# A GpSimd multiply ahead of the root, and one VectorE instruction per token tile, in the norm stages of a two-block transformer kernel

## What is computed

```python
def rms_norm(x, g):
    xf = x.astype(jnp.float32)
    y = xf * lax.rsqrt(jnp.mean(xf * xf, axis=-1, keepdims=True) + NORM_EPS)
    return (y * g.astype(jnp.float32)).astype(x.dtype)

        x = x + 0.5 * gt1 * rms_norm(swiglu(h, ...), g_post_ffn1[l])
        u = rms_norm(x, g_pre_mix[l]) * (1 + sc2) + sh2
        ...
        x = x + gt2 * rms_norm(y, g_post_mix[l])
        h = rms_norm(x, g_pre_ffn2[l]) * (1 + sc3) + sh3
        x = x + 0.5 * gt3 * rms_norm(swiglu(h, ...), g_post_ffn2[l])
```

## Time and profile before

| | us |
|---|---|
| median of 3 runs | 3116.41 |
| lowest, highest | 3114.98, 3118.16 |
| profiled execution, whole time | 3118.21 |
| profiled execution, span from first to last instruction | 3116.3 |
| mean granted TensorE clock of it, share of full speed | 0.957 |

### The profile page before, as it was taken

The page is one execution under the profiler, slowest core; times in us unless marked ns, Lnnn a source line. Parts: engine busy times, 40 slices in busy tenths (PEclk is TensorE's granted clock), DMA queues, the critical chain, the costliest instruction groups (busy, mean ns, idle before and its releaser), DMA issues. The chain is left out here.

```text
span 3116.3 us, 37658 instructions
## 1 busy us (share of the span) xinstructions
PE 2863.7 (92%) x14102; PEld 2417.8 (78%) x14102; DVE 2013.6 (65%) x3480; ACT 1072.6 (34%) x1575; POOL 923.7 (30%) x614
## 2 busy tenths in 40 slices
PE   4999997987789799997988699999999999999998
PEld 4788885875467688886865579999989999898776
DVE  6773755546842533334535359989588989898887
ACT  1321214224342422223225234655523333333333
POOL 0000000004221000000003134766767777776230
PEclk9999997988899899998998899999999999999999
DMA  7774731200023133331300124566789889888995
GB/s 277 243 255 149 242 122 68 92 26 16 21 68 101 54 108 99 90 101 48 103 13 8 68 84 140 173 191 195 253 330 330 324 327 331 300 335 310 351 348 195
DMA packets 298428, 536.70 MB, mean 172 GB/s; under 512 B 12600, under 2 KB 193180, under 8 KB 280476
## 3 DMA queue, kind: packets, MB, share of 16 engines
q1 hardware_dynamic: 211712, 375.07, 35.3%
q0 software_dynamic: 36864, 134.23, 11.9%
q10 hardware_dynamic: 49692, 25.28, 2.9%
HBM read 495.73 MB, written 38.80 MB: 172 GB/s over the span
## 5 line engine op out<-in xcount | busy, mean ns | idle before, releaser
L173 PE MATMUL ps<-query_h_hi,expert_u_hi 128*128 128x384 f32 (+1 forms) x1152 | 399.6, 347 | 1.9 <-ACT expert_u_hi L2302 1.0
L173 PE MATMUL ps<-query_h_lo,expert_u_hi 128*128 128x384 f32 (+1 forms) x1152 | 395.5, 343 | 0.0
L2041 POOL TENSOR_TENSOR expert_u_lo<-feat,expert_u_hi 128x1024 fp32r<-128x1024 f32 x142 | 349.1, 2460 | 124.2 <-ACT expert_u_hi L2302 122.9
L173 PE MATMUL ps<-expert_v_hi,expert_w_hi 128*128 128x512 f32 x768 | 303.8, 396 | 11.3 <-DVE expert_w_lo L2209 8.7
L173 PE MATMUL ps<-expert_v_hi,expert_w_lo 128*128 128x512 f32 x768 | 301.7, 393 | 0.0
L173 PE MATMUL ps<-expert_v_lo,expert_w_hi 128*128 128x512 f32 x768 | 301.3, 392 | 0.0
L2214 DVE TENSOR_TENSOR expert_v_lo<-peer_s,expert_v_hi 128x1024 fp32r<-128x1024 f32 x128 | 208.2, 1627 | 125.5 <-ACT expert_v_hi L2310 122.6
L173 PE MATMUL ps<-ffn_h_hi,ffn_w_hi 128*128 128x512 f32 x704 | 279.1, 396 | 7.4 <-DVE ffn_h_lo L636 5.8
L173 PE MATMUL ps<-ffn_h_hi,ffn_w_lo 128*128 128x512 f32 x704 | 276.6, 393 | 0.0
L173 PE MATMUL ps<-ffn_h_lo,ffn_w_hi 128*128 128x512 f32 x704 | 276.4, 393 | 0.0
L221 DVE TENSOR_TENSOR ffn_w_lo<-ffn_w_raw,ffn_w_hi 128x2048 fp32r<-128x2048 f32 x66 | 151.1, 2290 | 151.3 <-ACT ffn_w_hi L217 151.3
(11 more groups left out here) (452 smaller groups left out, 6480.7 us busy)
## 6 DMA issues: line engine op xcount, KB each, us to landing
feat<-in_expert_u_blocks SPq DMA_DIRECT2D x64, 1024.0 KB
peer_s<-in_expert_v_blocks SPq DMA_DIRECT2D x64, 1024.0 KB
gate_rows<-expert_gates SPq DMA_DIRECT2D x31, 768.0 KB
ffn_w_raw<-in_w_gate SPq DMA_DIRECT2D x44, 512.0 KB, 4.0
ffn_w_raw<-in_w_up SPq DMA_DIRECT2D x44, 512.0 KB, 5.3
ffn_w_raw<-in_w_down SPq DMA_DIRECT2D x22, 1024.0 KB, 4.9
gate_rows<-in_w_mod SPq DMA_DIRECT2D x18, 1024.0 KB, 6.4
in_w_raw<-in_w_in SPq DMA_DIRECT2D x16, 1024.0 KB, 5.1
```

The lines of the kernel that those rows point to most:

```text
L173: return nc.tensor.matmul(out, lhsT, rhs, start=start, stop=stop, skip_group_check=True)
L2041: nc.gpsimd.tensor_tensor(u_lo[:, n % 2, :, :], u_raw[:, n // 2 % 2, n % 2, :, :], u_hi[:, n % 2, :, :], ALU.subtract).then_inc(u_lo_done, 1)
```

## The change

In the three stages with a post-norm, tiles 1 to 3 get their gate row from GpSimd: `gate_tiles` multiplies `tok` by the row in place, as soon as ScalarE has summed the squares of that tile. VectorE then has one instruction for such a tile in place of two: `tok` times the reciprocal plus the residual, written to the residual. Tile 0 keeps the old pair. ScalarE takes three roots of `tok` up front and not two. A new semaphore, `pool_gated`, tells VectorE that a tile is multiplied.

```diff
+    def gate_tiles(pool):
+
+        for i in range(1, TT):
+            pool.wait_ge(tok_squares, i + 1)
+            nc.gpsimd.tensor_tensor(b.tok[:, i, :], b.tok[:, i, :], b.rows[:, post_row, :], ALU.mult).then_inc(pool_gated, 1)
+
...
+        if post_row is not None:
+            @block.gpsimd
+            def _(pool):
+                gate_tiles(pool)
...
             if post_row is not None:
                 tok_root(0)
                 tok_root(1)
+                tok_root(2)
...
-                if post_row is not None and i + 2 < TT:
-                    tok_root(i + 2)
+                if post_row is not None and i + 3 < TT:
+                    tok_root(i + 3)
...
-                nc.vector.scalar_tensor_tensor(b.tok[:, i, :], b.tok[:, i, :], b.post_stat[:, i:i + 1],
-                                               b.rows[:, post_row, :], ALU.mult, ALU.mult).then_inc(gated, 1)
-                dve.wait_ge(gated, i + 1)
-                nc.vector.tensor_tensor(b.x[:, i, :], b.x[:, i, :], b.tok[:, i, :], ALU.add).then_inc(added, 1)
+                if i == 0:
+                    nc.vector.scalar_tensor_tensor(b.tok[:, i, :], b.tok[:, i, :], b.post_stat[:, i:i + 1],
+                                                   b.rows[:, post_row, :], ALU.mult, ALU.mult).then_inc(gated, 1)
+                    dve.wait_ge(gated, 1)
+                    ins = nc.vector.tensor_tensor(b.x[:, i, :], b.x[:, i, :], b.tok[:, i, :], ALU.add)
+                else:
+                    dve.wait_ge(pool_gated, i)
+                    ins = nc.vector.scalar_tensor_tensor(b.x[:, i, :], b.tok[:, i, :], b.post_stat[:, i:i + 1], b.x[:, i, :],
+                                                         ALU.mult, ALU.add)
+                ins.then_inc(added, 1)
```

More of the change, by code:

```diff
@@ L542, in stage_norm_turn @@
     gated = b.sem(f"{tag}_gated")
+    pool_gated = b.sem(f"{tag}_pool_gated")
     added = b.sem(f"{tag}_added")
```

## The result

| | before | after |
|---|---|---|
| median, us | 3115.21 | 3120.66 |
| lowest to highest, 20 runs each | 3112.83 to 3120.25 | 3117.71 to 3123.83 |
| span of the profiled execution | 3116.3 | 3116.3 |

The changed kernel takes 1.0016 times as long, with a 95% interval of 1.0009 to 1.0023: it is slower by 5.45 us, by the interval 2.8 to 7.2. That is inside the forecast range and on the forecast side, 5 us under the forecast of 3125.7. The profiled execution of after happens to be among its shortest, so its span says nothing; what follows is read inside the stages.

What follows compares the result with a forecast made beforehand. The prediction took VectorE's chain to bound the three stages. It summed 3.5 us for the first stage and 2 x 2.9 for the others to 9.3, on 3116.4: 3125.7 us, range 3119 to 3130.

Steps and rivals of the forecast that it cites:

- VectorE's list is the bound: In the three stages VectorE's 18.47 us chain delays the first evacuation; a microsecond on it is one of the program.
- Exclusion by whole instructions: In the stages, GpSimd's multiplies and VectorE's large two-SBUF-input instructions take turns whole; nothing overlaps.
- The price of a multiply: Each GpSimd gate multiply of a full tile was taken as 2.41 us, from a subtraction of the same size.
- The short multiply: Rival for the GpSimd multiplies: 1.9 us each, stages lose 3.6 us in sum, 3120.0 us; chance 0.06.
- Two GpSimd instructions in a row do not let VectorE in between.: Later stages: tile 0's add waits for GpSimd's first and second multiplies, ending 4.43 us late.
- The race of the third multiply: Later stages: GpSimd's third multiply and VectorE's tile 2 instruction are issued 0.02 us apart; the order decides the path.
- fork (a): Later stages: VectorE's tile 2 instruction precedes GpSimd's third multiply; +2.9 us a stage, +2.2 with scaling free; chance 0.47.
- The scaling is kept out too: Later stages: VectorE's scaling of tile 1 is held by GpSimd's multiply, 0.7 us a stage above the free case.
- The first stage, +3.5 for the configuration change: First stage: GpSimd's first configuration change keeps it from starting before 496.8, making the stage 3.5 us longer.
- fork (b): Rival, later stages: GpSimd's third multiply precedes VectorE's tile 2 instruction; +3.8 us a stage, 11.3 in all, 3127.7; chance 0.37.
- What follows each stage has the same data in the same order, so nothing gives it back.: Behind each stage: none of the predicted 9.3 us loss is recovered.
- no exclusion: Rival: GpSimd's multiplies run beside VectorE's add and scaling; 5.4 us less, 3111.0, or 3109.4 with a hidden configuration change; chance 0.10.

Runs made afterwards that it cites:

- short_list: The changed kernel without GpSimd's multiplies, tiles 1 to 3 never multiplied by the gate row; 3104.88 against 3114.95 us for the kernel before, ratio 0.9965.
- beside: The kernel before plus three unneeded GpSimd multiplies of 128x1024 in each of the three stages, into a free buffer; 3133.23 against 3114.95 us, ratio 1.0058.
- the probes: The kernel before with an added block running GpSimd instructions against VectorE instructions issued at varied moments; in 90 cases the engines alternated, no program time given.
- turns_probe: The kernel before plus a block of GpSimd two-input multiplies, then one-input ones, beside VectorE instructions; 30 small adds took 0.80 to 2.28 us.
- early_gpsimd: The kernel before with only tile 1's gate multiply on GpSimd, at the very start of the stage; 3114.80 against 3114.95 us, ratio 0.9998.
- again: The changed kernel once more, on another chip, against the kernel before; 3119.95 against 3116.26 us, ratio 1.0014.
- early_vector: The kernel before with VectorE multiplying tiles 0 and 1 by the gate row while it waits for the first root; 3111.75 against 3114.95 us, ratio 0.9985.

## Why the prediction held, step by step

- **VectorE's list is the bound, and a microsecond on it is one of the program.** Right. short_list took 2.91 us a stage off (8.7 in three) and the program took 10.1 less; beside added 5.92 a stage (17.8) and the program took 18.3 more. For the changed kernel itself the two do not agree as well, 7.4 against 5.45 and 3.7; see below.
- **Exclusion by whole instructions.** Right, in both directions, in all three stages and in the probes. It outweighs the removed adds: 5.83 us held for 3.7 removed. The prediction's sentence that every two-input instruction found under a GpSimd one of two inputs was held is too wide, though: it holds for two inputs in SBUF (see the last section).
- **The price of a multiply.** Right: 2.33 to 2.36 us where VectorE does not hold it up, predicted 2.41. The "2.41 again" by way of the half-size add was no second piece of evidence, since the fixed 0.17 had been worked out from the 2.41. The short multiply falls, and with it the rival whose number, 3120.0, happens to lie next to the result.
- **"Two GpSimd instructions in a row do not let VectorE in between."** Wrong, and this is the step that failed. It was read from one pair and made the add of tile 0 4.43 us late; it is 2.03 late, because it got its turn between the first multiply and the second. No row of before showed a turn between two GpSimd instructions or spoke against it: the earlier trace rows have one GpSimd instruction with none pending behind it. The earlier trace rows were read rightly, and what they show recurs at that place in every profile; but it does not hold in the norm stage, and one place was not enough for a rule.
- **The race of the third multiply.** It did not take place. With the add 2.4 us earlier than the walk had it, tile 1's instruction was the second to be held, and the third multiply was issued while that one stood, ahead of tile 0's scaling. Neither fork was right; the total held, 5.83, is what three turns of about 1.9 to 2.0 give. That the stage still lost 2.46, near fork (a)'s 2.9, is in part luck: two multiplies in one wait had been counted, and three single waits came. Of the signs named ahead, an add of 5.6 us and a first evacuation after 21.3 to 22.3 us did not come (3.26, and 20.93).
- **The scaling is kept out too.** Right as a rule, at another place: tile 0's scaling, 2.65 for 0.75, and 2.76 in beside. The earlier trace rows did not speak against it, because there GpSimd had one input; turns_probe measured that case apart, and found 1.53 where GpSimd's multiply gives 2.65.
- **The first stage, +3.5 for the configuration change.** Wrong: it is like the others, +2.46. The sign named ahead for this, a first stage that loses as the others do, came. The change stands at 490.5, and the first multiply starts at 494.37, 0.07 after the sum of squares of tile 1 is there (494.11 + 0.19). In that run up to 3.9 us could still lie hidden in between; early_gpsimd leaves 0.1. The 5.5 us of the earlier trace rows were then the wait for `dil_inverse` alone, and the change is at the lower end of the bound. The Trainium skill (GPSIMD Engine Reference, section Instruction dispatch) counts about 6 us for the first call of newly loaded code; in early_gpsimd none of it is seen ahead of this multiply. Whether any code was newly loaded there, no trace tells.
- **The sum.** 9.3 was predicted; the stages lose 3 x 2.46 = 7.4. Of the 1.9 us between them, 1.0 is the first stage and 0.9 the other two. The medians lose 5.45 and, in again, 3.7. The prediction had set 6.2 us, 0.2%, as the least that can be told from no change, and 5.45 is less than that; with 20 runs of each kernel the interval, 2.8 to 7.2, excludes no change. In fork (b) the first stage stands at 3.65 with no working; by the main sum's 3.5 the rival would be at 3127.5.
- **"What follows each stage has the same data in the same order, so nothing gives it back."** Not quite. The order is the same, but the moment at which TensorE's clock rises is not. The third stage, first product behind the evacuation and the products around the rise of the clock, in after:

```profile
1477.54 0.76 PE L173 MATMUL ps<-in_w_hi,in_h_hi 128*128 128x512 f32 x1 [2.65 <-DVE in_h_lo L654]
...
1479.81 0.63 PE L173 MATMUL ps<-in_w_hi,in_h_lo 128*128 128x512 f32 x1
1480.24 0.48 PE L173 MATMUL ps<-in_w_hi,in_h_hi 128*128 128x512 f32 x1
1480.56 0.39 PE L173 MATMUL ps<-in_w_lo,in_h_hi 128*128 128x512 f32 x1
```

Before, the granted clock stands near half of full in the stages, which is the 1.2 GHz level, and it is 0.50 in after too while these first products run (1477.5 to 1480.2); there a product of 128x512 takes 0.63 us and the next starts 0.43 later. At full clock it takes 0.39 and the next starts 0.23 later. In after the first product at full clock of the third stage comes 5.47 us after the evacuation, behind 7 at the lower one; before it was 7.63 us (1470.51 to 1478.14), behind 12. Five products fewer at the lower clock, at 0.20 us each (0.43 less 0.23), are 1.0 us given back there. In the first two stages the counts are 11 and 12 after, 9 and 11 before, which costs 0.6. For again the counts are 8, 13 and 7, a sum of 28 against 32 before, and so again about 0.8 given back. That is 0.4 and 0.8 us of the single executions that were profiled; it shows how far the stages' ends move from one execution to the next, and is not shown to be a cause of the difference between the medians. Between the stages' 7.4 and the medians' 5.45 and 3.7 there remain 2.0 and 3.7 us that I have not found. The intervals (2.8 to 7.2 and 1.6 to 7.2 us) end just short of 7.4. All that lies outside the three stages takes 3060.9 us in the profile of before, 3053.5 in after and 3058.5 in again; in short_list, beside, early_gpsimd and early_vector, where the instructions outside are the same, 3056.3 to 3059.4. So single executions differ there by several us; after is the lowest of them all, and again lies among the kernels that changed nothing there. Whether anything outside the stages answers to the change is left open.

Both errors (two multiplies in one wait, and the configuration change in the first stage) made the forecast too high, and the range reached far enough down, to 3119, to hold them. What carried the sign was the exclusion; its rival, no exclusion, is ruled out by the held rows of all three stages and of beside.

## What to carry to other kernels

GpSimd is no spare engine for float32 tensors of two inputs while VectorE is the bound: where VectorE's list consists of instructions with two SBUF inputs and of such scalings, each GpSimd instruction takes nearly its whole time out of that list, less what VectorE had idle anyway. Moving 1.2 us of VectorE's work to a 2.3 us GpSimd multiply loses, unless the multiply lies where VectorE idles; where there is such idle time, VectorE can use it itself at half the price, as early_vector does. And a rule on who gets in first should rest on more than one pair of rows, and on rows of the same kind of place, since whole forks of a walk hang on it.

## What the runs showed of the hardware

- **Turns.** With two tensor inputs on GpSimd (128x1024, float32), VectorE's instructions of two SBUF inputs and its float32 scaling of one wait for GpSimd's end, and GpSimd waits for theirs. At each boundary the other engine is let in if it has something pending, even if it was issued 0.07 us before: 90 cases in the probes, and in the stages of the changed kernel too. The exception is the VectorE instruction near 2260 us, which stands through two GpSimd instructions in every profile. A held wide instruction of two inputs ends about 1.09 us after GpSimd's end, a multiply about 2.2 after VectorE's. The Trainium skill (SBUF — State Buffer, section Who interferes with whom) describes the shared pair of ports as a lock for the whole instruction, with the faster two-port form of the scaling among those that take it; these rows agree with that.
- **An input in PSUM is not held.** The kernel before has 96 VectorE instructions of two inputs, 128x1024, of which one is in PSUM (`ps`). Many lie beside GpSimd instructions of two inputs, one from 1972.10 beside a subtraction that runs from 1971.18 to 1973.58, and none of the 96 takes over 1.23 us:

```profile
L2185 DVE TENSOR_TENSOR peer_hots<-peer_lists_t,ps x48: 1214/1215/1223, 1947.1 to 2221.2; 128x1024 f32<-128x1024 f32 x48
```

- **One input on GpSimd is another case.** By the Trainium skill (SBUF — State Buffer, section Who interferes with whom) an instruction of VectorE with two SBUF inputs contends with a GpSimd instruction that reads SBUF, and contention is an exclusive lock. Here the measurement decides otherwise: with a one-input multiplication on GpSimd, VectorE's two-input instructions took 1.21 to 1.23 us as ever. The scaling was slowed from 0.75 to 1.53 and not held to GpSimd's end, and GpSimd from 2.75 to 3.75, so the engines do get in each other's way, but neither is shut out.
- **The return of TensorE's clock scatters.** In the profiled executions of the kernels here, the first product at full clock came from 5.5 to 8.5 us after the first evacuation, behind 7 to 14 at the lower clock. At 0.20 us for a product, that is up to 1.4 us between two stages with the same instructions, more than half of the 2.46 us that the change cost a stage.
